# One joined stage for adaLN, norms and QKV, and one for SSD input and SSD, in a float32 two-block kernel

## The reference

```python
# adaLN: shift, scale and gates from c (tokens) and c_ctx (context), silu(c) @ w_ada + b_ada
h  = modulate(rmsnorm(x, g), shift, scale)        # 512 tokens; hc likewise for 256 context tokens
q, k, v, z, xbc, dt_raw, gates = split(h @ w_in)  # hc: k, v, xbc, dt
o = differential_attention(q, [kc, k], [vc, v])
# SSD: xbc -> depthwise conv of 3 taps -> silu -> xs, B, C ; dt = softplus(dt_raw + bias)
# per direction (forward, backward), 16 heads of 64, state 128, from h0 = 0 over the context,
# whose last state starts the scan over the tokens:
acum   = cumsum(dt * a)
states = einsum(B, exp(acum[-1] - acum) * dt, x)          # one chunk's contribution
h_next = h * exp(acum[-1]) + states
y      = (C @ B^T * decay * dt) @ x + C @ h_prev * exp(acum)
```

## Time and profile before

| | |
|---|---|
| time, median of 3 runs | 3980.57 us (3980.3 to 3980.94) |
| the profiled execution, its own time | 3985.6 us |
| its span | 3983.8 us |
| mean granted TensorE clock | 0.933 |
| TensorE (PE) busy | 3569.8 us, 90% |
| VectorE (DVE) busy | 1586.6 us, 40% |
| ScalarE (ACT) busy | 1418.0 us, 36% |
| GpSimd (POOL) busy | 1200.6 us, 30% |

### The profile page before, as it was taken

How to read it: one execution, slowest core, us unless ns; L and a number is a source line. 1 busy time by engine, 2 the same in 40 slices (tenths; PEclk the granted TensorE clock), 3 DMA queues, 4 the chain that set the end, 5 groups by cost and what they waited for, 6 DMA issues and landing times. The chain is left out here.

```text
span 3983.8 us, 44202 instructions
## 1 busy us (share of the span) xinstructions
PE 3569.8 (90%) x17344; PEld 2744.1 (69%) x17344; DVE 1586.6 (40%) x2223; ACT 1418.0 (36%) x1744; POOL 1200.6 (30%) x559
## 2 busy tenths in 40 slices
PE   4989987779959999999638999998999999799999
PEld 1886576567845666666427777776788878678887
DVE  2216633642137666666542333333521231243212
ACT  3215432234233555555133434343422231133221
POOL 0430021543411333333014333231244433134443
PEclk7999998889979999999869999998999998589999
DMA  4322211002216999999722222221122211012322
GB/s 166 104 66 85 85 43 43 1 22 87 102 46 224 343 349 355 356 362 364 280 76 88 68 70 74 68 71 64 65 95 95 95 64 64 0 43 106 105 96 74
DMA packets 94478, 494.53 MB, mean 124 GB/s; under 512 B 21646, under 2 KB 21902, under 8 KB 43760
## 3 DMA queue, kind: packets, MB, share of 16 engines
q1 hardware_dynamic: 74496, 452.75, 31.9%
q0 software_dynamic: 19824, 39.54, 2.8%
HBM read 470.18 MB, written 40.89 MB: 128 GB/s over the span
## 5 line engine op out<-in xcount | busy, mean ns | idle before, releaser
L268 PE MATMUL ps<-arena_r,arena_r 128*128 128x512 f32 x2080 | 845.1, 406 | 42.2 <-POOL ring_r L259 24.9
L269 PE MATMUL ps<-arena_r,arena_r 128*128 128x512 f32 x2080 | 817.5, 393 | 0.0
L259 POOL TENSOR_TENSOR ring_r<-ring,arena_r 128x2048 fp32r<-128x2048 f32 x100 | 464.3, 4644 | 937.5 <-ACT arena_r L255 937.5
L255 ACT ACTIVATE arena_r<-ring 128x2048 fp32r<-128x2048 f32 x166 | 316.7, 1909 | 565.9 <-PE ps L270 410.1
L268 PEld LDWEIGHTS ps<-arena_r,arena_r 128*128 128x128 f32 x2080 | 395.3, 190 | 147.3 <-issue 53.1
L269 PEld LDWEIGHTS ps<-arena_r,arena_r 128*128 128x128 f32 x2080 | 395.6, 190 | 88.9 <-issue 11.1
L259 POOL TENSOR_TENSOR arena_r<-ring,arena_r 128x2048 fp32r<-128x2048 f32 x66 | 304.1, 4607 | 414.3 <-ACT arena_r L255 414.3
L270 PE MATMUL ps<-arena_r,arena_r 128*128 128x512 f32 x1056 | 411.1, 389 | 0.0
L270 PE MATMUL ps<-arena_r,ring_r 128*128 128x512 f32 x1024 | 406.0, 396 | 0.0
L1770 DVE TENSOR_TENSOR arena_r<-arena,arena_r 128x2048 fp32r<-128x2048 f32 x132 | 301.8, 2288 | 171.0 <-ACT arena_r L1728 167.5
L1728 ACT ACTIVATE arena_r<-arena 128x2048 fp32r<-128x2048 f32 x132 | 250.1, 1910 | 128.0 <-DMA arena<-we_gu 104.9
(11 more groups left out here) (373 smaller groups left out, 6158.5 us busy)
## 6 DMA issues: line engine op xcount, KB each, us to landing
ring<-wstream SPq DMA_DIRECT2D x193, 1024.0 KB, 4.9
arena<-we_gu SPq DMA_DIRECT2D x132, 1024.0 KB
arena<-we_down SPq DMA_DIRECT2D x66, 1024.0 KB, 7.3
arena<-ys SPq DMA_DIRECT2D x32, 512.0 KB, 8.5
arena<-arena SPq DMA_DIRECT2D x192, 64.0 KB, 2.0
arena<-arena SPq DMA_DIRECT2D x32, 128.0 KB, 4.8
arena<-x_t SPq DMA_DIRECT2D x1, 2048.0 KB, 10.1
h<-arena SPq DMA_DIRECT2D x1, 2048.0 KB, 6.6
```

The costliest lines, as they stand in the source:

```text
L255: act.activation(whalf(c, 0), ring[:, c % NSLOT, :], ACT.Copy).then_inc(sem("chunk_hi"), 1)
L259: pool.tensor_tensor(whalf(c, 1), ring[:, c % NSLOT, :], whalf(c, 0).bitcast(F32), ALU.subtract).then_inc(sem("chunk_lo"), 1)
L268: pe.matmul(out, hi, rhs[0], start=start, stop=False)
L269: pe.matmul(out, hi, rhs[1], start=False, stop=False)
```

## The change

Four edits.

1. adaLN, both norms and QKV become one phase. SP loads vec and cst, then three chunks, then x and the context, and the four tables after the eighth chunk. The squares and their sums run beside adaLN's products; the first half of the rows is copied and turned after the sixth chunk, the square sums are made after the seventh. VectorE normalises all 16 tiles by itself (no scale, no shift); scale and shift follow once mod is there, on VectorE for the even token tiles and on ScalarE for the others, each just ahead of its split.
2. SSD input and SSD become one phase. The sums' exponentials come before the last two SiLUs; the rebuild and the skip term come behind the context's states.
3. The context's states no longer run as a recurrence of four steps. Each of the two tiles is turned once, weighted per direction by dt times decay to the end (times the other tile's whole decay for the tile that comes first), and both products of a direction accumulate in one pair of PSUM banks, which VectorE copies to STATE[d].
4. In the loop over the eight token steps VectorE makes the differences of the first half before it adds the last step's state, and masks the next step's C B^T before it waits for the output. All chains of VectorE use one semaphore (`dve_link`).

```diff
+        def first_sync(sp):
+            for dst, src in ((vec[:, :], vecs), (cst[:, :, :], consts)):
+                sp.dma_start(dst, src).then_inc(sem("loaded"), 16)
+        def tokens_sync(sp):
+            sp.dma_start(XT, x_t).then_inc(sem("x_loaded"), 16)
+            sp.dma_start(view(R, KT, TC), ctx_t).then_inc(sem("ctx_loaded"), 16)
...
+        def tables_sync(sp):
+            for dst, src in ((rope[:, :, :], rope_t[0]), (gmask[:, :, :], gmask_t), (wdt[:, :, :], w_dt),
                              (wrt[:, :, :], w_router)):
-                sp.dma_start(dst, src).then_inc(sem("loaded"), 16)
+                sp.dma_start(dst, src).then_inc(sem("tables_loaded"), 16)
...
             act.wait_ge(sem("lam_dots"), 1)
             act.activation(small[:, 2:4], small[:, 0:2], ACT.Exp).then_inc(sem("lam_exp"), 1)
+            for x, n, m in TOKENS:
+                act.wait_ge(sem(("x_loaded", "ctx_loaded")[m]), 16)
+                for k in range(KT):
+                    if k >= 2:
+                        act.wait_ge(sem("st_acc"), 7 * m + max(1, k - 2))
+                    act.activation(SQS[m][k % 2], x[:, k, :], ACT.Square).then_inc(sem("st_sq"), 1)
+            act.wait_ge(sem("chunk_done"), CH_ADA + 4)
+            act.activation(ADA_OUT[:, 0:D], ADA_ROWS[:, 0:D], ACT.Copy).then_inc(sem("ada_rows"), 1)
+            for x, n, m in TOKENS:
+                act.wait_ge(sem("st_sums"), m + 1)
+                act.activation(RSTD[m], bank(6 + m, n), ACT.Ln, scale=1.0 / D, bias=epst[:, :]).then_inc(sem("st_ln"), 1)
+                act.wait_ge(sem("st_ln"), m + 1)
+                act.activation(RSTD[m], RSTD[m], ACT.Exp, scale=-0.5).then_inc(sem("st_rs"), 1)
             act.wait_ge(sem("chunk_done"), CH_ADA + 8)
...
+            act.activation(ADA_OUT[:, D:2 * D], ADA_ROWS[:, D:2 * D], ACT.Copy).then_inc(sem("ada_rows"), 1)
+            chunk_hi(act, CH_QKV)
...
+                if n == 5:
+                    turn(0)
+                if n == 6:
+                    for x, w, m in TOKENS:
+                        pe.wait_ge(sem("st_acc"), 7 * m + 7)
+                        pe.matmul(bank(6 + m, w), C["ones"], SQ_TOTAL[m], start=True, stop=True).then_inc(sem("st_sums"), 1)
+            turn(1).then_inc(sem("ada_turned"), 1)
...
+            for x, n, m in TOKENS:
+                for k in range(1, KT):
+                    dve.wait_ge(sem("st_sq"), 8 * m + k + 1)
+                    if k >= 2:
+                        dve.wait_ge(sem("st_acc"), 7 * m + k - 1)
+                    dve.tensor_tensor(SQ_TOTAL[m], SQS[m][0] if k == 1 else SQ_TOTAL[m], SQS[m][k % 2],
+                                      ALU.add).then_inc(sem("st_acc"), 1)
+            for x, n, m in TOKENS:
+                dve.wait_ge(sem("st_rs"), m + 1)
+                for k in range(KT):
+                    dve.tensor_tensor((HT, HC)[m][:, k, :], x[:, k, :], RSTD[m], ALU.mult).then_inc(sem("st_normed"), 1)
...
+            ins.then_inc(sem("ada_gain"), 1)
...
-        HC = view(R, KT, TC)
-        norm(XT, T, HT, lambda k: gain[:, A1 + k:A1 + k + 1], lambda k: mod[:, k, 0:1])
-        norm(HC, TC, HC, lambda k: gain[:, A1 + 8 + k:A1 + 9 + k], lambda k: mod[:, k, 1:2])
...
+        def shifted_vector(dve, i):
+            a, b = affine(i)
+            dve.wait_ge(sem("st_normed"), i + 1)
+            dve.wait_ge(sem("ada_gain"), 1)
+            dve.tensor_scalar(QX.src[i], QX.src[i], a, b, ALU.mult, ALU.add).then_inc(sem("st_full_v"), 1)
+        def shifted_scalar(act, i):
+            a, b = affine(i)
+            act.wait_ge(sem("st_normed"), i + 1)
+            act.wait_ge(sem("ada_gain"), 1)
+            act.activation(QX.src[i], QX.src[i], ACT.Identity, scale=a, bias=b).then_inc(sem("st_full_s"), 1)
...
-            for k in range(KT):
-                QX.high(act, k)
+            for i in range(0, KT, 2):
+                shifted_scalar(act, i + 1)
+                full_high(act, i)
+                full_high(act, i + 1)
             chunk_hi(act, CH_QKV + 1)
-            for k in range(KT, 2 * KT):
-                QX.high(act, k)
+            for i in range(KT, 2 * KT):
+                shifted_scalar(act, i)
+                full_high(act, i)
...
+            pool.wait_ge(sem("tables_loaded"), 64)
...
+            for i in range(0, KT, 2):
+                shifted_vector(dve, i)
+                if i:
+                    QX.low(dve, i - 2)
+                    QX.low(dve, i - 1)
+            for i in range(KT - 2, 2 * KT):
                 QX.low(dve, i)
...
+                if ch == 7:
+                    dt_sums_scalar(act)
...
+                if ch == 7:
+                    dt_sums_vector(dve)
...
                 ins = XX.rebuild(dve, k)
-            link(ins)
+            ins.then_inc(sem("xbc_rebuilt"), 1)
...
-            act.activation(flat(DECAY), bank(7, 192), ACT.Exp)
+            act.activation(flat(DECAY), bank(7, 192), ACT.Exp).then_inc(sem("dt_exps"), 1)
...
-        STEPS = [(0, 0), (1, 1), (0, 1), (1, 0), (0, 2), (1, 5), (0, 3), (1, 4), (0, 4), (1, 3), (0, 5), (1, 2)]
-        NCTX = 4
...
+        STEPS = [(0, 2), (1, 5), (0, 3), (1, 4), (0, 4), (1, 3), (0, 5), (1, 2)]
+        CONTEXT = [(t, d) for t in range(2) for d in range(2)]
...
+        CXW = (XW, XDT)
+        CBTOK = (BTOK, CBM.rearrange("p a b -> p (a b)"))
...
+                else:
+                    pe.wait_ge(sem("xbc_silu"), 8)
+                    pe.wait_ge(sem("xbc_taps"), 8)
...
+                if m == 0:
+                    pe.wait_ge(sem("ssd_cstate"), q + 1)
+                elif q == 1:
                     pe.wait_ge(sem("ssd_y"), m)
...
+            def context_state(t, d):
+                pe.wait_ge(sem("ssd_cxw"), 2 * t + d + 1)
+                if d == 0:
+                    pe.wait_ge(sem("ssd_btok"), t + 1)
+                if t == 0 and d == 0:
+                    pe.wait_ge(sem("xbc_taps"), 8)
+                    pe.wait_ge(sem("dt_exps"), 1)
+                for g in range(SSD_G):
+                    mm = pe.matmul(bank(4 + 2 * d + g // 2, 256, (g % 2) * 256), CBTOK[t][:, g * P:g * P + P],
+                                   CXW[d][:, g * 256:g * 256 + 256], start=(t == 0 and g % 2 == 0), stop=(t == 1),
+                                   skip_group_check=True)
+                mm.then_inc(sem("ssd_cstatemm"), 1)
...
+            pe.wait_ge(sem("xbc_silu"), 6)
+            pe.wait_ge(sem("xbc_taps"), 7)
+            for t in range(2):
+                if t:
+                    pe.wait_ge(sem("ssd_cxw"), 2)
+                    pe.wait_ge(sem("ssd_btok"), 1)
+                turn(t, t, True)
+                for d in range(2):
+                    context_state(t, d)
             inner(0)
             for q in range(2):
                 rows(0, q)
-            for n in range(NCTX, len(STEPS)):
-                m = n - NCTX
-                turn(n)
-                if n + 1 < len(STEPS):
+            for m in range(len(STEPS)):
+                if m:
+                    pe.wait_ge(sem("ssd_state"), min(m, NSTATE))
+                    pe.wait_ge(sem("ssd_btok"), min(m + 2, NSTATE + 2))
+                else:
+                    pe.wait_ge(sem("ssd_cxw"), 4)
+                    pe.wait_ge(sem("ssd_btok"), 2)
+                turn(m + 2, STEPS[m][1], m < NSTATE)
+                if m + 1 < len(STEPS):
                     inner(m + 1)
                 output(m)
...
+            dve.wait_ge(sem("dt_exps"), 1)
+            link(dve.tensor_tensor(WCOL, DT[:, :, 0:2, :], TOEND[:, :, 0:2, :], ALU.mult))
+            for d in range(2):
+                ins = dve.tensor_tensor(WCOL[:, d, d, :], WCOL[:, d, d, :], DECAY[:, d, 1 - d, :], ALU.mult)
+            link(ins)
+            for t, d in CONTEXT:
+                dve.wait_ge(sem("ssd_xturn"), t + 1)
+                if t:
+                    dve.wait_ge(sem("ssd_cstatemm"), d + 1)
+                dve.tensor_tensor(split(CXW[d], SSD_H, 64), split(pf[:, 0:1024], SSD_H, 64), hcol(WCOL[:, d, t, :]),
+                                  ALU.mult).then_inc(sem("ssd_cxw"), 1)
+            for d in range(2):
+                dve.wait_ge(sem("ssd_cstatemm"), d + 3)
+                dve.tensor_copy(STATE[d], bank(4 + 2 * d, 1024)).then_inc(sem("ssd_cstate"), 1)
+            rebuild_vector(dve)
+            mask_inner(0)
+            for m, (d, t) in enumerate(STEPS):
+                differences(m, 0)
+                if 1 <= m <= NSTATE:
+                    add_state(m - 1)
+                differences(m, 1)
+                dve.wait_ge(sem("ssd_xturn"), m + 3)
+                if m:
...
+                if m + 1 < len(STEPS):
+                    dve.wait_ge(sem("ssd_decay"), 2 * m + 2)
+                    mask_inner(m + 1)
+                dve.wait_ge(sem("ssd_ymm"), m + 1)
+                y = Y[:, :, (t - 2) * P:(t - 1) * P]
+                dve.wait_ge(sem("ssd_skip"), 1)
```

(18 more changed lines are left out.)

281 lines of the change are left out of this document (147 added, 134 removed).

## The result

The changed kernel takes 3894.74 us (median of 4 runs, 3892.36 to 3897.23) against 3980.76 us for the kernel before (4 runs, 3980.3 to 3983.09): a ratio of 0.9783, 95% interval 0.9766 to 0.98, or 86.0 us less. The forecast was 3902.6, with 3893 to 3916 as its range. The profiled execution took 3896.65 us.

What follows compares the result with a forecast made beforehand. TensorE was busy 92 to 95% of two untouched long stretches; serial chains bound the beginning, GpSimd's chain the SSD loop. −40 −24 −14 = −78 off the median 3980.57 gave 3902.6 us, range 3893 to 3916.

Steps and rivals of the forecast that it cites:

- beginning: Loads, adaLN, norms and first QKV chunk: that chunk ends at 72.5 instead of 112.4 us, −40 us, bounds −46 and −33.
- head: Start of the SSD, up to the first mask: mask at 690.3 instead of 714.32 us, −24 us, bounds −21 and −27.
- loop: SSD token steps: period 15.75 instead of 18.2 us, about 1 us given back at the end; −14 us, bounds −7 and −17.
- last stretch: Everything behind the SSD, which the change leaves alone: no gain, 3 us allowed either way for where the clock falls.
- (b): adaLN's weight chunks: the token loads delay chunk 3, TensorE idles 5 us, and adaLN ends only 1.3 us sooner.
- (e): First QKV chunk: shifts and splits pace TensorE from 60 to 66.8, its second half ends near 72.2 us.
- (d): VectorE's normalising before QKV: GpSimd's split holds the port 4.5 us, one context tile waits, ending near 57.4 us.
- triangle of step 0: SSD head, GpSimd at 659 to 663 beside VectorE's taps: costs nothing; up to 3.6 us if it collided.
- R1: SSD loop: GpSimd's triangle gets the port before VectorE's SCALED, period 17.0, loop −7, total −71, 3910 us; chance 0.14.
- R2: SSD loop does not speed up, the output product holding the period at 18.2: total −64, 3916 us; chance 0.08.
- R3: Beginning: token loads starve adaLN, which ends 6 to 10 us later than 47.9: total −70, 3911 us; chance 0.13.
- R4: Last stretch: less rest lowers the granted clock from 0.94; below 0.915 the change loses; chance 0.02.

Runs made afterwards that it cites:

- e4: The kernel before with only the SSD part of the change, keeping its old adaLN, norms and QKV: 3943.63 us, ratio 0.9906 to the kernel before.
- e3: The changed kernel with SSD input and SSD as two stages again, a barrier between them: 3901.74 us, ratio 0.9811 to the kernel before.
- e1: The kernel before with edit 4 alone, the new order of VectorE's work in the token loop: 3965.9 us, ratio 0.9963 to the kernel before.
- e2: The changed kernel with edit 4 undone, so the loop has its old order: 3911.51 us, ratio 0.983 to the kernel before.
- e8: The changed kernel with one wait added, so VectorE scales the state only after GpSimd's next triangle: 3906.8 us, ratio 0.9826 to the kernel before.
- e5: The changed kernel with x and the context loaded behind the fourth weight chunk instead of the third: 3902.57 us, ratio 0.9814 to the kernel before.

## Why the prediction was right

The forecast was the likeliest case of the prediction, and each of its three terms has its place in the traces. In changes to the profile of before:

| | forecast | measured | undone or alone |
|---|---|---|---|
| beginning | -40 (-46 to -33) | -42.2 (112.53 to 70.29); at P -43.0 | -43.1 (e4) |
| head | -24 (-27 to -21) | -24.6 | of which 2.8 the joining (e3) |
| loop | -14 (-17 to -7) | -15.4 | -12.8 alone (e1), -13.7 undone (e2) |
| last stretch | 0 (3 either way) | -6.9 in the profiles; -3.8 is what the medians leave to it | follows no edit (D) |
| sum | -78 | -89.0 in the spans, -86.0 in the medians | |

The measured gain is 8 us larger than the forecast. The three terms give 4.2 of these, 2.2 at the beginning, 0.6 in the head and 1.4 in the loop; the other 3.8 us have no cause in the change, and it is by them that the result lies near the fast end of the range (3893). The prediction's own bounds hold a slip: −93 has the 3 us of the last stretch in it, −61 has not, and with them it is −58.

**Beginning.** The chain was the forecast's, and its terms were off by a few microseconds that partly cancelled, which is luck. The gap ahead of the fourth chunk was 2.08 us where (b) had 5: the loads ran at 427 GB/s from 8.65 to 23.39, not at the 359 of the first 19.3 us. That chunk and the two behind it took 10.52 us and not 12.2, since the clock did not fall in so short a gap (0.219 us a record). So adaLN ended at 44.37 and not 47.9, 3.5 sooner. Against that (e) had TensorE follow the splits, and it began at the lower level (0.50 granted from 56.16 to 60.81): its 48th product ends at 69.48, 13.3 us after the first started, where the forecast had 12.2. ScalarE, splitting the context's tiles without a gap, reaches the copy another 0.8 us later. (d) put the port's collision on a context tile; it fell on GpSimd's split and then on the gains, but cost VectorE what was said, about 4 us. The mis-sized term is the transfer's rate. The slow first records were read rightly as the lower level's pace, although gives 1.00 for 19.30 to 23.00: the trace's first record of the clock is at 23.57, and there the records go from 0.43 to 0.22 us; in the changed kernel it is at 13.02, with the same step.

**Head.** It is 24.6 against 24, and the steps are the forecast's: B's copy and not VectorE released the first product, the first tile took 5.76 us (5.7), VectorE's copies, rebuilds and skips follow in the order given. That the triangle of step 0 collides with nothing held; e3 shows what it costs where it does.

**Loop.** The period is 15.87 (15.75), six times 2.38 is 14.3, and the 1 us that the last two steps were to give back was not given back: from the last triangle to the last addition to Y it is 18.2 us in both, and the first mask to the first full triangle is 0.9 shorter (9.4 to 8.5).

**Rivals.** R1 is priced right and does not occur (e8). R2 is refuted by e1 and e2. R3 did not happen, adaLN ended 3.5 us before the forecast's time and not 6 to 10 behind it; its mechanism holds in small, since the transfer is not hidden and moves with its place in the queue (e5), but at 427 GB/s the gap is 2 us. R4 is refuted by the last stretch's clock, 0.94 in both kernels. What the trace does not settle is the 4 to 7 us of the last stretch. It lies between the extremes of that stretch in kernels that all leave it alone (3122.7 to 3136.4, before 3132.2), so I take it for scatter; it was not tested by itself, since no edit touches it.
